# The first norm of two transformer layers: factor applied behind the projections, tiles turned one at a time, last down products and the store in halves

## The reference, cut to what matters

```python
def rms_norm_2(x, g):
    y = x * lax.rsqrt(jnp.mean(x * x, axis=-1, keepdims=True) + EPS)
    return y * g

x = first_block(x, ...)      # ends with x = x + rms_norm(conv_ffn(...), ffn_post_norm)
for l in range(2):
    x = x + token_mixer(rms_norm_2(x, norm_mix[l]), w_in[l], ...)
    x = x + peer_ffn(rms_norm_2(x, norm_ffn[l]), ...)
```

## Time and profile before

| | us |
|---|---|
| median of 3 runs (2305.91 to 2306.96) | 2305.94 |
| the profiled execution, its own time | 2305.72 |
| its span | 2303.9 |
| TensorE busy | 2036.8 (88%) |
| VectorE busy | 1628.7 (71%) |
| ScalarE busy | 1147.3 (50%) |
| GpSimd busy | 846.1 (37%) |

### The profile page before, as it was taken

The page is one execution under the profiler, slowest core; times in us unless marked ns, Lnnn a source line. Parts: engine busy times, 40 slices in busy tenths (PEclk is TensorE's granted clock), DMA queues, the critical chain, the costliest instruction groups (busy, mean ns, idle before and its releaser), DMA issues.

```text
span 2303.9 us, 30543 instructions
## 1 busy us (share of the span) xinstructions
PE 2036.8 (88%) x10119; PEld 1353.7 (59%) x10162; DVE 1628.7 (71%) x3313; ACT 1147.3 (50%) x2531; POOL 846.1 (37%) x574
## 2 busy tenths in 40 slices
PE   9999999999999899887778788999899987878777
PEld 8999899998998744432222233999754432223222
DVE  4565777776776877777677776776877777677776
ACT  5454455555454555544444445455555544444453
POOL 0000011100010256556666663020256565666663
PEclk9999999999999999999999999999999999999999
DMA  7533466665535799999999999534799999999997
GB/s 244 166 128 118 137 188 202 199 189 194 176 114 177 273 412 421 421 421 421 422 421 419 422 422 367 179 120 167 263 408 420 421 422 421 421 422 421 422 422 327
DMA packets 120994, 710.41 MB, mean 308 GB/s; under 512 B 14016, under 2 KB 14272, under 8 KB 54720
## 3 DMA queue, kind: packets, MB, share of 16 engines
q0 software_dynamic: 76992, 546.34, 57.5%
q1 hardware_dynamic: 41744, 151.60, 20.8%
q10 hardware_dynamic: 2160, 11.17, 1.2%
HBM read 708.02 MB, written 4.19 MB: 309 GB/s over the span
## 4 chain that ended last, share of the span: by engine, by line
PE 43%; DMA 24%; POOL 10%; issue 8%; DVE 8%; ACT 6%; DVEq 0%; POOLq 0%; ACTq 0%
DMA work<-in_experts,expert_idx 23%; PE ps L477 10%; POOL work L986 10%; PE ps L479 10%; PE ps L478 10%; PE ps L1172 7%; PE ps L615 2%; DVE weights_lo L462 2%; DVE work L1856 2%; PE ps L593 1%; PE ps L583 1%; ACT L1461 1%; ACT weights_hi L457 1%; ACT L1405 1%; ACT arena L1466 1%
## 5 line engine op out<-in xcount | busy, mean ns | idle before, releaser
L1172 PE MATMUL ps<-work,arena 128*128 128x512 f32 x2048 | 999.7, 621 | 224.0 <-ACT arena L1466 223.1
L986 POOL DMA_INDIRECT work<-in_experts,expert_idx x512 | 794.1, 1551 | 598.6 <-PE ps L1172 316.0
L1856 DVE CUSTOM_DVE_ANT_0 work<-h_norm,work 128x1024 f32<-128x1024 f32 x512 | 627.5, 1226 | 323.3 <-DMA work<-in_experts,expert_idx 318.4
L1172 PEld LDWEIGHTS ps<-work,arena 128*128 128x128 f32 x2048 | 363.9, 193 | 835.0 <-ACT arena L1466 530.9
L462 DVE TENSOR_TENSOR weights_lo<-weights,weights_hi 128x1024 fp32r<-128x1024 f32 x286 | 354.6, 1246 | 181.9 <-ACT weights_hi L457 181.3
L477 PE MATMUL ps<-feat_hi,weights_hi 128*128 128x256 f32 x1576 | 459.8, 292 | 6.4 <-DVE weights_lo L462 2.0
L457 ACT ACTIVATE weights_hi<-weights 128x1024 fp32r<-128x1024 f32 x286 | 301.7, 1057 | 323.4 <-PE ps L479 281.0
L1461 ACT ACTIVATE small<-small 128x1 f32<-128x1 f32 x512 | 150.1, 293 | 607.5 <-DVE small L1856 607.0
L478 PE MATMUL ps<-feat_lo,weights_hi 128*128 128x256 f32 x1576 | 446.4, 283 | 0.0
L479 PE MATMUL ps<-feat_hi,weights_lo 128*128 128x256 f32 x1576 | 446.3, 283 | 0.0
L477 PEld LDWEIGHTS ps<-feat_hi,weights_hi 128*128 128x128 f32 x1576 | 302.8, 192 | 16.9 <-issue 8.2
(11 more groups left out here) (209 smaller groups left out, 1729.9 us busy)
## 6 DMA issues: line engine op xcount, KB each, us to landing
weights<-in_wstream SPq DMA_DIRECT2D x286, 512.0 KB, 3.8
work<-in_experts,expert_idx POOLq DMA_INDIRECT x512, 14.6
arena<-in_wstream POOLq DMA_DIRECT2D x12, 512.0 KB, 6.4
na_rows<-in_rpb POOLq DMA_DIRECT2D x32, 96.0 KB, 4.5
arena<-na_rows ACTq DMA_DIRECT2D x2, 1536.0 KB, 10.1
params<-in_par ACTq DMA_DIRECT2D x2, 1476.0 KB, 6.8
arena<-in_bias ACTq DMA_DIRECT2D x5, 512.0 KB, 4.7
params<-in_par ACTq DMA_DIRECT2D x1, 1024.0 KB, 6.3
```

The lines of the kernel that those rows point to most:

```text
L986: nc.gpsimd.indirect_dma_start(ring[:, r, :], None, experts, bass.IndirectOffsetOnAxis(ap=EIDX[:, b, c * RING + r:c * RING + r + 1], axis= ...
L1172: ins = nc.tensor.matmul(bank(2 * t + h), DIAG[:, r, :], ring[:, r, D + h * 512:D + (h + 1) * 512], start=False, stop=False)
L1856: nc.vector.tensor_tensor_reduce(ring[:, r, 0:D], HN[:, t, :], ring[:, r, 0:D], 1.0, 0.0, ALU.mult, ALU.add, hd[:, r:r + 1]).then_inc(dots ...
```

## The change

1. Last down halves (`last_down`): both halves are waited for first, then the products run by tile and column half, each of the four with its own signal (`ff_tile`). Squares, gain, factor and update of x (`square_half`, `gained_half`, `root_of`, `factor_of`, `normed_half`) go by tile and half.
2. Start of a layer: x itself is turned, by tile and pairs of chunks (`mix_turn`, `mix_hi`, `mix_lo`), without the factor. Tile 0 is turned as soon as it is there: in layer 0 while tile 1 is being normed, in layer 1 within the last expert step of layer 0. The first group's first half is split in advance and multiplied tile by tile. The squares and the factor come after `split_hi` of half 2.
3. The factor is the scale of `take2` for groups 0 to 8 (one activation for each tile). For the gates, whose tokens lie along the free dimension, the factor is laid on all partitions by a matmul of ones with two diagonals (before group 5), and VectorE multiplies each gate group by it (`gate_mult`) ahead of ScalarE's bias.
4. Loads: the first 24 columns of the parameters are loaded in the feed-forward network or in the expert stage; the bias rows of layer 0 after x is complete; the first weight half of layer 1 without a wait for the last gather.
5. Expert stage: the last two steps of tile 1 are written out; tile 0's x is added in the step before the last, by halves; the last step picks nothing ahead. The last pick closes each bank by itself.
6. Store in three parts: tile 0 after the last gather landed, tile 1's left and right half when each is added.

```diff
+        def mix_turn(pe, l, t, b):
+            pe.wait_ge(*((x_left, 2 * l + t + 1) if b < 2 else (x_ready, 3 * l + TT + 1 + t)))
+            if t and b % 2:
+                pe.wait_ge(n_mix.hT, 8 * l + b + 1)
+            for c in range(2):
+                ins = nc.tensor.transpose(mix_turned(t, b)[:, c, :], X[:, t, (2 * b + c) * P:(2 * b + c + 1) * P], ident)
+            ins.then_inc(n_mix.xp, 1)
+        def expert_sum(dve, l, t, side):
+            dve.wait_ge(acc_ready, 3 * l + 1 + (t and 1 + side))
+            dst, src = half_of(t, side)
+            nc.vector.tensor_tensor(dst, dst, src, ALU.add).then_inc(x_ready if side else x_left, 1)
...
# SyncE
-                if n >= L_HALF + L_HALVES and local < SLOTS:
+                if n >= L_HALF + L_HALVES and 0 < local < SLOTS:
                     sp.wait_ge(g_landed[RING - 1], l * USES * 16)
-            sp.dma_start(out.rearrange("(t p) d -> p t d", p=P), X[:, :, :]).then_inc(out_stored, 16)
+            sp.dma_start(out[0:P, :], X[:, 0, :]).then_inc(out_stored, 16)
+            sp.wait_ge(x_left, (LAYERS + 1) * TT)
+            sp.dma_start(out[P:S, 0:HB], X[:, 1, 0:HB]).then_inc(out_stored, 16)
# TensorE, start of a layer
-                keep_warm(pe, 5)
-                norm_pe(pe, n_mix, l)
+                if l == 0:
+                    for b in range(4):
+                        mix_turn(pe, l, 0, b)
+                    w = split_pe(pe, L_HALF, at)
+                    first_tok(w, 0, 0, range(HC))
+                    keep_warm(pe, 2, 7)
+                    mix_turn(pe, l, 1, 0)
+                    mix_turn(pe, l, 1, 1)
+                else:
+                    mix_turn(pe, l, 1, 0)
+                    mix_turn(pe, l, 1, 1)
+                    w = split_pe(pe, L_HALF, at)
+                    first_tok(w, 0, 0, range(HC))
+                first_tok(w, 0, 1, range(HC)).then_inc(half_done, 1)
+                mix_turn(pe, l, 1, 2)
+                mix_turn(pe, l, 1, 3)
+                w = split_pe(pe, L_HALF + 1, at)
+                for t in range(TT):
+                    ins = first_tok(w, 1, t, range(HC, KC))
# ScalarE, start of a layer
+                mix_hi(act, l, 1, 0)
+                mix_hi(act, l, 1, 1)
+                if l == 0:
+                    act.wait_ge(x_ready, 2 * TT)
+                    load_rest(0)
+                split_hi(act, L_HALF + 1, at)
+                mix_hi(act, l, 1, 2)
+                mix_hi(act, l, 1, 3)
+                split_hi(act, L_HALF + 2, at)
+                for t in range(TT):
+                    ins = nc.scalar.activation(junk[:, t, :], X[:, t, :], ACT.Square, accum_out=ssq[:, t:t + 1])
+                nc.scalar.activation(std, ssq, ACT.Sqrt, scale=1.0 / D, bias=eps_col).then_inc(n_mix.std, 1)
+                act.wait_ge(n_mix.rstd, l + 1)
+                for t in range(TT):
+                    ins = nc.scalar.activation(HN[:, t, 0:P], ident, ACT.Copy, scale=rstd[:, t:t + 1])
# VectorE, start of a layer
+                mix_lo(dve, l, 1, 0)
+                mix_lo(dve, l, 1, 1)
+                split_lo(dve, L_HALF + 1, at)
+                mix_lo(dve, l, 1, 2)
+                mix_lo(dve, l, 1, 3)
+                split_lo(dve, L_HALF + 2, at)
+                dve.wait_ge(n_mix.std, l + 1)
+                nc.vector.reciprocal(rstd, std).then_inc(n_mix.rstd, 1)
                 dve.wait_ge(par2_loaded, l * 16 + 16)
                 dve.wait_ge(na_loaded, l * 16 + 16)
                 ch.step(nc.vector.tensor_tensor(na4, na4, ..., ALU.add))
+                def gate_mult(g):
+                    dve.wait_ge(half_done, at.halves + L_HALF + 2 * g + 2)
+                    dve.wait_ge(factor_taken, l + 1)
+                    nc.vector.tensor_tensor(GT[:, f:f + 2, :], bank(6 + g % 2)..., view(factor, [0, 2], [1, S]), ALU.mult)
```

More of the change, by code:

```diff
@@ L245, in build @@
         junk = HN
+        eps_col = SMALL[:, 306:307]
+        ones, factor = before[:, 0:P], not_before
+        HB = D // 2
         def bank(b, n=1):
@@ L1057, in _, with down @@
             norm_pe(pe, n_ffn, 0)
-            def down(n, at, gated, last):
+            def down(n, at, gated):
                 for j in range(2):
@@ L1063, in down @@
                         for h in range(2):
-                            ins = product(bank(2 * t + h), cols((FGH[:, j, :], FGL[:, j, :]), t * P, P), cols(w, h * 512, 512),
-                                          False, last and j == 1)
+                            ins = product(bank(2 * t + h), cols((FGH[:, j, :], FGL[:, j, :]), t * P, P), cols(w, h * 512, 512), False, False)
                     ins.then_inc(half_done, 1)
@@ L1076, in _ @@
                     group_fm(pe, G_FF + 2 + j, 6 + j, at)
-                down(F_HALF + 8, at, i * 2, False)
-            down(L_HALF - 2, 0, FF_BLOCKS - 2, True)
-            keep_warm(pe, 6)
+                down(F_HALF + 8, at, i * 2)
+            last_down = []
+            for j in range(2):
+                pe.wait_ge(ff_gated, FF_BLOCKS - 1 + j)
+                last_down.append(split_pe(pe, L_HALF - 2 + j))
+            for t in range(TT):
+                for h in range(2):
+                    for j in range(2):
+                        ins = product(bank(2 * t + h), cols((FGH[:, j, :], FGL[:, j, :]), t * P, P), cols(last_down[j], h * 512, 512), False, j == 1)
+                        if (t, h, j) == (1, 1, 0):
+                            ins.then_inc(half_done, 1)
+                    ins.then_inc(ff_tile, 1)
@@ L1082, in _, with first_tok @@
+            pe.wait_ge(ff_tile, 4)
+            pe.sem_inc(half_done, 1)
             for l in range(LAYERS):
                 at = At(l, L_HALVES, HELD_TURNS)
-                keep_warm(pe, 5)
-                norm_pe(pe, n_mix, l)
+                def first_tok(w, h, t, chunks):
+                    for c in chunks:
+                        if c % 2 == 0:
+                            pe.wait_ge(n_mix.hT, 8 * l + 4 * t + c // 2 + 1)
+                        ins = product(ps[:, 6 * 512 + t * GC:6 * 512 + (t + 1) * GC], feat(c, t * P, P), cols(w, c % HC * GC, GC),
+                                      False, c == KC - 1 and t == TT - 1)
+                    return ins
+                nc.tensor.matmul(bank(6), ZERO[:, 0:P], ZERO[:, :], start=True, stop=False)
+                if l == 0:
[17 more added lines that the diff above has]
+                    ins = first_tok(w, 1, t, range(HC, KC))
+                ins.then_inc(half_done, 1)
@@ L1381, in _ @@
                         take2(g)
+                        if g == 5:
+                            act.wait_ge(factor_done, l + 1)
+                            nc.scalar.activation(factor, bank(5)[:, 0:S], ACT.Copy).then_inc(factor_taken, 1)
                         g += 1
```

241 lines of the change are left out of this document (180 added, 61 removed).

## The result

| | us |
|---|---|
| kernel before, median of 7 runs beside the changed one (2303.86 to 2309.17) | 2305.94 |
| changed kernel, median of 7 runs (2310.83 to 2319.18) | 2315.43 |
| ratio, with its 95% interval | 1.0038 (1.0028 to 1.0047) |
| profiled execution of the changed kernel, its own time / its span | 2315.1 / 2313.3 |
| TensorE, VectorE, ScalarE, GpSimd busy | 2036.5 (88%), 1611.2 (70%), 1150.8 (50%), 856.9 (37%) |

The change makes the kernel slower by 0.38%, 9.5 us between the medians and 9.4 between the spans of the two profiled executions. The forecast was 2309.1, range 2299 to 2314: wrong, with the measured time 1.4 above the range's upper end.

The account below looks back on a forecast made before the run. The prediction took TensorE to bound a layer and the gathers an expert stage. Terms +2.0 + 2.3 + 3.0 + 1.25 - 3.2 - 2.2 = +3.15 on 2305.94 gave 2309.1 us, range 2299 to 2314.

Parts of the forecast that it names:

- Layer 0's start: Half 3's split waits behind the mask addition and bias rows; TensorE idles from 575.9 to 581.8: +2.0 and +2.3 us.
- the clock low behind it: After TensorE's idle time in layer 0, half of a low-clock stretch is lost: +2.3 us, bounds 0 and 3.4.
- the term of +2.0: Layer 0's half 3 starts at 581.8 against 579.85 before: +2.0 us, bounds -1.2 and +4.2.
- The wait at queries and keys: Two gate products on VectorE precede the copies TensorE waits for: +0.9 to 1.0 us in each layer.
- The other six products: Six more gate products on VectorE lie in its waits for probabilities: 0; if none were covered, 4.1 us.
- The end: Last half added sooner and a smaller last store, -0.35 and -1.9: -2.2 us, bounds -2.7 and -1.5.
- the estimate beside it: By the Trainium skill's 2.0 us fixed per DMA, the last store half lands after 2.6; end term -1.7.
- Layer 1's half 3: Starts 18.8 us after the last gather's landing, 22.0 before: -3.2, bounds -6.6 and -2.5.
- I leave it out and price it below: Layer 1's start: TensorE idles 3.4 us before half 3, the clock taken to hold, so no clock loss in the sum.
- the rival "Slower": The clock also falls at layer 1's start: +2.3 us, 2311.4; chance of slower by the clock 0.26.
- The longer form of that rival: The clock falls already while x is turned, keep-warm products take twice as long: +2 more, 2313.5; no separate chance.
- the early load: Layer 1's first weight half, loaded in layer 0's expert stage, delays the gathers: +1.25 us, bounds 0 and 1.3.

Follow-up runs that it names:

- e7: e1 with the store of the kernel before, one transfer of 1 MB: 2305.04 us, ratio 0.9999 to the kernel before.
- e3: Changed kernel with TensorE multiplying zeros between half 2 and half 3 of each layer: 2309.69 us, ratio 1.0022 to the kernel before.
- e1: Changed kernel with both layers' mask addition moved on VectorE behind the split of half 6: 2302.29 us, ratio 0.9989 to the kernel before.
- e8: e1 with all three first weight halves of layer 1 loaded without the wait for the last gather: 2307.27 us, ratio 1.0009 to the kernel before.
- e6: Kernel before with its mask addition moved on VectorE in the same way as in e1: 2305.17 us, ratio 0.9998 to the kernel before.
- e10: Kernel before with tile 1's last two steps on VectorE and ScalarE, and TensorE's last, written out behind the loops: 2309.81 us, ratio 1.0021.
- e12: Kernel before with TensorE's last step alone written out, VectorE and ScalarE keeping their loops: 2306.50 us, ratio 1.0010 to the kernel before.

## Why the prediction was wrong

**Right, in kind and nearly in size.** Layer 0's start: half 3 held by the mask addition behind the bias rows, TensorE idle for 5.9 (5.75), the clock low behind it (+2.3; 2.6 for half 3 alone). Half 3 starts 22.45 behind the last down product where it was 21.7, so the term of +2.0 was +0.75: the issue of the bias rows came earlier than forecast (562.81, not 567.1, of which 2.3 are the earlier end of the first block), the landing after 10.9 instead of 9.8. The wait at queries and keys: +0.9 to 1.0 a layer; it was +1.1 and +0.6. The other six products: 0. The end: -2.2; it was -2.5, of which e7's trace gives 2.0 to the parts of the store, for 1.9. A part of 256 KB landed after 2.0, where the sum had 2.1 and the estimate beside it 2.6. Layer 1's half 3 at 18.8 after the last landing; it was 19.3.

**The step that failed: "I leave it out and price it below".** The forecast kept the clock full behind 3.4 us of idle time in layer 1, by its nearness to the 1.94 and 2.04 of rows 8. The idle time was 4.21 and the clock fell, +2.3 for half 3 alone. That was the rival "Slower" (2311.4), which still leaves 4.0 to the measured 2315.4. In the profiles of this study idle times of 3.6 to 5.8 at this place were followed by a low clock in 6 of 6 places, those up to 1.2 in none, and e3 shows that it is the idleness. The bracket from rows 8 was read as open between 2.04 and 7.5; the middle of it should not have gone to the optimistic end. It was not even open: the trace of before has a wait of 2.82 in the first block, with a low clock for 3.4 us behind it.

```profile
280.61 0.66 PE L407 MATMUL ps<-consts,h_norm 128*128 128x128 f32 x4 [2.82 <-ACT h_norm L340]
```
```profile
281.50:284.90 3.40, 3.40 (x18) 3.34 (x17) 2.73 (x7) 2.88 (x8) 0.00 (x0) 0.50 0.00 0
```

Nor do two waits of one execution make a rule. In the first block, ahead of everything that was changed, the clock fell behind the wait of 1.94 at 209 in 7 of the 14 profiles, behind the one of 1.80 to 2.04 at 243 in 4 and behind the 2.82 at 280 in 6.

The longer form of that rival (the clock falls while x is turned), and with it what the Trainium skill says on transposes (TensorE: Matmul & The Clock Gate, "Part 4: PE-mode transpose"), was not seen at the start of a layer: in e1 the clock is full behind the same pairs of transposes. At the turn of queries and keys, where eight transposes stand between the two waits, the 5 of 10 low clocks fit the rule, but no run tells it there from two waits that add up.

**What no rival had, first:** that the longer wait at queries and keys could also bring the clock down: +3.0 and +1.5 in the profiled execution, in half of the cases over all profiles. The forecast priced the wait, 0.9 to 1.0, and not what it can trigger. A third wait of this kind is in no term either: the last down products now wait 2.0 for both gated halves (1.15 before), and behind that the clock was low for 3.4 us in 4 of the 9 changed kernels that leave the wait idle, the changed kernel itself not among them.

**Second:** the steps written out behind the loops. The forecast costed their work (covered, rightly) and the early load (+1.25; the second 32 picks of stage 0 took 81.6 on average in the nine changed kernels other than e8 and 80.3 in the kernel before, e6, e10 and e12, +1.3). It gave the form of the code no price: one late landing more, 0.97, at the end of each stage, 4.5 in e10's median. Stage 1, which has no early load, was 1.6 longer and showed this. Stage 0 was only 0.9 longer in this execution; in the eight other changed kernels, e8 left out and cut in the same way, it was 633.6 to 636.1, where the kernel before, e6 and e12 have 632.2.

**Summed,** by the table's stretches, measured less forecast: first block -2.3, layer 0's start with the second wait at queries and keys -0.9, the clock behind that wait +3.0, to the experts -0.4, stage 0 -0.3, layer 1's first part +4.8, its second +1.0, stage 1 +1.6, end -0.3. That is +6.2, and with the forecast's +3.15 the +9.4 seen. Of layer 1's 4.8, half 3 starts 0.5 later than forecast, the clock behind it is 2.3 in half 3 and some 0.8 in half 4 (granted clock 0.72 from 1455 to 1460), the clock behind queries and keys 1.5, the wait there 0.3 less than forecast. The +1.0 behind it is a wait of TensorE for VectorE that layer 0 has in both kernels and layer 1 only in the changed one. It is not of the change: e10 and e12 have it in layer 1 too (0.93 and 0.90), e6 half of it.

## What to carry to other kernels

When a change brings work forward, look at what else stands in the queue ahead of it: an operation that waits for a load (the mask addition) was harmless while the start was late and cost 13 us once it was early; moved behind the splits it made nothing wait. Price each lengthened wait of TensorE twice, for itself and for the clock behind it. Look through the whole trace for waits of about that length, not at two of them, and don't take a clock that held once for one that holds: behind the same wait it fell in one execution and not in the next. Zeros in the gap tell waiting and clock apart in one run. Writing out the last steps of a loop is not free, even with no work added.

## What the runs showed of the hardware

- TensorE's granted clock fell to 1.2 GHz behind idle times of 3.6 to 5.8 us in 6 of 6 places, behind single waits of 1.94, 1.80 to 2.04 and 2.82 in the first block in 7, 4 and 6 of 14 profiles, behind two waits of 0.83 to 1.36 and 1.26 with eight transposes between them in 5 of 10, and behind 0.78 to 0.85 (once 1.31) and 0.66 to 0.69 in 0 of 18. With products of zeros in 5.35 of 5.7 us it stayed full.
- A 512 KB load into a stage that is bound by gathers cost about 1.3 us for the first one, its bytes at 421 GB/s (1.25), and by the median some 2.5 for each of e8's two more, twice that (2.3 by its stage).
- In every kernel some landings of a stage come 3.4 us or more behind the one before instead of 2.5, 103 of 104 of them within 4 us behind an 8 KB instruction packet. Steps written out behind the loops of VectorE and ScalarE went with such a landing, late by 0.97, among the last 32 gathers of every stage that had such steps, and none came there in those that had not.
